# A hybrid pooling and state-space layer: state-space blocks projected first, the scan in two halves of groups, tables on VectorE, the output projection in two passes

## The reference, cut to what matters

```python
h = rmsnorm(x) * (1 + sc1) + sh1                  # sc1, sh1, g1, sh2, sc2, g2: silu(cond) @ w_ada
proj = h @ w_in                                   # 1024 -> 512 pooling channels, 512 state-space channels
pool_out = [(window_mean(u_g, w) - u_g) @ pool_w[g] for w in (2, 4, 8, 16)] * pool_scale
# state space: 32 groups of 16 channels, 64 complex states, one scan in each direction
bu = einsum("gnp,blgp->blgn", b_bar, u);  h_t = a_bar * h_{t-1} + bu_t
y = gelu(D * u + Re(C_f h_f) + Re(C_b h_b));  ssm_out = y * sigmoid(y @ w_glu)
x = x + g1 * (concat(pool_out, ssm_out) @ w_out)
x = x + g2 * (square(relu(norm(x) @ w_mlp1)) @ w_mlp2)
return rmsnorm(x), final context states
```

## Time and profile before

| | |
|---|---|
| median of three runs | 1408.06 us (1408.01 to 1409.33) |
| the profiled execution | 1408.4 us, span from first to last instruction 1406.6 us |
| TensorE | 1265.9 us busy, 90% of the span, mean granted clock 0.951 |
| VectorE | 909.6 us busy |
| GpSimd | 625.9 us busy |
| ScalarE | 306.4 us busy |
| chain that ended last | TensorE 73%, GpSimd 12%, VectorE, DMA and ScalarE 3% each |

### The profile page before, as it was taken

How to read it: one execution, slowest core, us unless ns; L and a number is a source line. 1 busy time by engine, 2 the same in 40 slices (tenths; PEclk the granted TensorE clock), 3 DMA queues, 4 the chain that set the end, 5 groups by cost and what they waited for, 6 DMA issues and landing times.

```text
span 1406.6 us, 18516 instructions
## 1 busy us (share of the span) xinstructions
PE 1265.9 (90%) x6399; PEld 1062.3 (76%) x6399; DVE 909.6 (65%) x1238; ACT 306.4 (22%) x595; POOL 625.9 (44%) x458
## 2 busy tenths in 40 slices
PE   3869997847788898899999999999999999999995
PEld 0269894104467786799899889989988998998893
DVE  1778689999944765884664565466456545645648
ACT  2462324002122311641011001101101110110113
POOL 1100412992103378524733653573375356337436
PEclk9879998877989999999999999999999999999998
DMA  8711366530484511020110111011001001101003
GB/s 208 257 30 31 112 132 106 185 119 1 75 254 69 173 30 46 16 90 23 53 60 30 30 60 45 15 60 60 29 30 60 31 28 60 59 17 43 30 0 134
DMA packets 82834, 101.63 MB, mean 72 GB/s; under 512 B 31974, under 2 KB 66442, under 8 KB 82412
## 3 DMA queue, kind: packets, MB, share of 16 engines
q1 hardware_dynamic: 62360, 85.59, 20.8%
q0 software_dynamic: 3136, 12.06, 3.3%
q10 hardware_dynamic: 17300, 3.48, 1.3%
HBM read 89.53 MB, written 9.49 MB: 70 GB/s over the span
## 4 chain that ended last, share of the span: by engine, by line
PE 73%; POOL 12%; DVE 3%; DMA 3%; ACT 3%; SPq 2%; issue 2%; ACTq 1%; POOLq 0%; DVEq 0%
PE bank L1088 21%; PE bank L1090 21%; PE bank L1089 21%; POOL acc L459 4%; POOL from_state L437 2%; POOL acc L469 2%; DMA raw<-in_w_ada 2%; POOL ca_tmp L434 2%; POOL from_state L432 2%; SPq L350 1%; PE bank L1101 1%; ACT h_tile L506 1%; PE bank L1205 1%; PE bank L1231 1%; ACTq L483 1%
## 5 line engine op out<-in xcount | busy, mean ns | idle before, releaser
L469 POOL TENSOR_TENSOR acc<-acc,gated 128x512 f32<-128x512 f32 x288 | 401.8, 1395 | 391.7 <-DVE gated L1052 352.7
L1088 PE MATMUL bank<-x_hi,w_hi 128*128 128x384 f32 x992 | 332.8, 335 | 0.0
L1089 PE MATMUL bank<-x_lo,w_hi 128*128 128x384 f32 x992 | 332.2, 335 | 0.0
L1090 PE MATMUL bank<-x_hi,w_lo 128*128 128x384 f32 x992 | 332.1, 335 | 0.0
L1052 DVE TENSOR_TENSOR gated<-bank,gate_b 128x512 f32<-128x512 f32 x288 | 194.4, 688 | 117.8 <-PE bank L1090 96.3
L1088 PE MATMUL bank<-w_hi,f_hi 128*128 128x512 f32 x576 | 224.4, 390 | 1.4 <-DVE w_lo L1033 0.8
L1090 PE MATMUL bank<-w_hi,f_lo 128*128 128x512 f32 x576 | 224.4, 390 | 0.0
L1089 PE MATMUL bank<-w_lo,f_hi 128*128 128x512 f32 x576 | 224.4, 390 | 0.0
L1042 DVE TENSOR_TENSOR f_tmp<-relu 128x384 f32<-128x384 f32 x96 | 65.5, 682 | 210.9 <-ACT relu L716 210.5
L716 ACT ACTIVATE relu<-bank 128x384 f32<-128x384 f32 x96 | 47.2, 493 | 649.0 <-PE bank L1090 647.3
L1088 PEld LDWEIGHTS bank<-x_hi,w_hi 128*128 128x128 f32 x992 | 186.8, 188 | 0.7 <-issue 0.2
(11 more groups left out here) (237 smaller groups left out, 1500.6 us busy)
## 6 DMA issues: line engine op xcount, KB each, us to landing
raw<-in_w_mlp SPq DMA_DIRECT2D x64, 512.0 KB, 3.6
raw<-in_w_ada SPq DMA_DIRECT2D x48, 512.0 KB, 5.0
x_tile<-in_x_sample POOLq DMA_DIRECT2D x8, 512.0 KB, 8.4
raw<-in_w_in SPq DMA_DIRECT2D x8, 512.0 KB, 4.0
raw<-in_w_out SPq DMA_DIRECT2D x8, 512.0 KB, 7.0
acc<-in_x_sample SPq DMA_DIRECT2D x1, 4096.0 KB, 13.5
out<-acc SPq DMA_DIRECT2D x8, 512.0 KB, 2.6
inv_count_b<-in_inv_count POOLq DMA_DIRECT2D x4, 576.0 KB, 4.4
```

The lines of the kernel that those rows point to most:

```text
L469: GP.tensor_tensor(a, a, BT[i % 4][:], ALU.add).then_inc(s.acc, 1)
L1088: mm(out, sh_, mh, start=first, stop=False)
L1089: mm(out, sh_, ml, start=False, stop=False)
L1090: return mm(out, sl, mh, start=False, stop=last)
```

## The change

- The input projection takes the four state-space blocks first (`IN_MB`), then the pooling blocks. The 32 groups are two halves of 16. The states of the first half are made behind the third block (VectorE evacuates every second pair), those of the second half behind the projection. The chunks keep the context's columns beside the latents', so their transfers are half as many.
- `to_state` and `from_state` are built on VectorE, eight calls each of three operations on 1024 elements. The transposition of the `to_state` blocks is spread over the projection (`WB_AT`).
- The scan runs once for each half; the seven single steps at the top become three folds with steps of 1, 2 and 4 (two more powers). Between the steps of the first scan VectorE splits weights; between those of the second it gates the blocks of the first output pass.
- The pooling windows run on VectorE between the two scans, in one padded buffer that ScalarE fills (`pad`), with the latents' and the context's sums in one operation up to the last level.
- A unit of conditioning is four matmuls of 256 columns, each on its own 32 rows of PSUM, and the bias comes as a ninth unit of each part. Parts 4 and 5 are spread over the first output pass.
- The output projection has two passes of four input blocks: pooling channels beside the second scan, state-space channels behind the GLU.
- The store of the outputs goes out in four parts, and `acc` is loaded in four.

Of the lines taken out none is shown below; they are the ones described in the section before.

```diff
+GB = G // 2
+KK_AT = 5
+WB_AT = {(1, 0): (0, 1), (1, 1): (2, 3), (1, 2): (4, 5), (2, 0): (6, 7),
+         (3, 0): (8, 9), (3, 1): (10, 11), (3, 2): (12, 13), (4, 0): (14, 15)}
...
+    W_OUT1, W_GLU, W_OUT2, W1 = N_IN, N_IN + N_HALF, N_IN + N_HALF + N_GLU, N_IN + 2 * N_HALF + N_GLU
...
+    IN_MB = [4, 5, 6, 7, 0, 1, 2, 3]
...
+        def load_u(b):
+            for i in range(2):
+                sp.wait_ge(uds[2 * b + i], 16)
+            ud = UD[b * GB * SP:(b + 1) * GB * SP, :].rearrange("(g p) t -> p g t", p=SP)
+            for j in range(L):
+                sp.dma_start(U[b][j * SP:(j + 1) * SP, :, :], ud[:, :, j * CH:(j + 1) * CH]).then_inc(u_in[b], 16)
...
+        def store_y(b, h):
+            sp.wait_ge(s.y_ev, 8 * b + 4 * (h + 1))
+            g0 = b * GB + 8 * h
+            for j in range(L):
+                sp.dma_start(yd[:, g0:g0 + 8, j * CH:(j + 1) * CH], Y[b][j * SP:(j + 1) * SP, 8 * h:8 * h + 8, :])\
+                  .then_inc(yd_w[b], 16)
...
+        for g, q in enumerate((s.yr0, s.yr1, s.yr2)):
+            for k in range(4):
+                dst = YR[:, k, :]
+                if g < 2:
+                    sp.dma_start(lat_j3(dst[:, g * TG:(g + 1) * TG]), yds[:, k, 3 * g:3 * g + 3, 0:CL]).then_inc(q, 16)
+                else:
+                    sp.dma_start(lat_j3(dst[:, 2 * TG:LAT]), yds[:, k, 6:8, 0:CL]).then_inc(q, 16)
+                    sp.dma_start(dst[:, LAT:T].rearrange("p (j c) -> p j c", c=CC), yds[:, k, :, CL:CH]).then_inc(q, 16)
...
+        load_counts(2)
+        turn_local(0)
+        load_counts(3)
...
+        for i in range(18):
+            if i in (0, 6, 10):
+                gp.wait_ge((s.acc_in0, s.acc_in1, s.acc_in2)[(0, 6, 10).index(i)], 16)
+            if i == 16:
                 gp.wait_ge(s.acc_ctx_in, 16 * L)
+            add_gated(i, BT3[i % 3])
+            if i == KK_AT:
+                turn_local(1)
...
+            if i == 2:
+                act.wait_ge(s.wbt, 8)
+                for p_ in range(0, 16, 2):
+                    states_out(p_)
...
+        pad(0)
+        for hf in range(2):
+            ada_row(2, hf)
+        pad(1)
+        kernels_out(0)
+        for hf in range(2):
+            ada_row(3, hf)
+            ada_col(3, hf)
+        pad(2)
+        for i in range(8):
+            y_out(0, i)
+        pad(3)
...
+        act.wait_ge(s.mix_pool, NG)
+        act.wait_ge(s.yd_w0, 16 * 2 * L)
+        kernels_out(1)
+        for hf in range(2):
+            ada_row(4, hf)
+            ada_col(4, hf)
+        for hf in range(2):
+            ada_row(5, hf)
+        for i in range(8):
+            y_out(1, i)
...
+        def to_state(b, d, h):
+            gs = slice(b * GB + 8 * h, b * GB + 8 * h + 8)
+            q0 = d * G + gs.start
+            out = WB[b][:, d, 8 * h:8 * h + 8, :].rearrange("n g (j p) -> n g j p", p=SP)
+            powers = [t_[:, L - 1::-1, q0:q0 + 8] if d == 0 else t_[:, 0:L, q0:q0 + 8] for t_ in (PR, PI)]
+            pr, pi = (t_.rearrange("n e q -> n q e").unsqueeze(3).to_broadcast([P, 8, L, SP]) for t_ in powers)
+            b1, b2 = (t_[:, q0:q0 + 8, :].unsqueeze(2).to_broadcast([P, 8, L, SP]) for t_ in (B1, BY))
+            tmp = TPQ[:, 0:8 * P].rearrange("n (g j p) -> n g j p", g=8, p=SP)
+            tt(tmp, b2, pi, ALU.mult).then_inc(s.dve, 1)
+            tt(out, b1, pr, ALU.mult).then_inc(s.dve, 1)
+            count[0] += 2
+            dve.wait_ge(s.dve, count[0])
+            tt(out, out, tmp, ALU.add).then_inc(s.wbt, 1)
...
+        def scan(b, between):
+            hb = H[b]
+            step = [0]
+
+            def folded(ins):
+                then(ins)
+                between(step[0])
+                step[0] += 1
...
+            for k in range(4):
+                folded(fold(b, 0, 4 * k, 4, slice(1, CH - 2, 2), slice(2, CH - 1, 2)))
+            for k in range(2):
+                folded(fold(b, 1, 8 * k, 8, slice(2, CH - 5, 4), slice(4, CH - 3, 4)))
+            folded(fold(b, 2, 0, GB, slice(4, CH - 11, 8), slice(8, CH - 7, 8)))
+            folded(fold(b, 3, 0, GB, slice(8, CL - 23, 16), slice(16, CL - 15, 16)))
+            then(V.memset(hb[:, :, :, CL], 0.0))
+            for i in range(3):
+                w = 16 << i
+                folded(fold(b, 4 + i, 0, GB, slice(0, CL - 15 - w, 16), slice(w, CL - 15, 16)))
+            folded(fold(b, 3, 0, GB, slice(0, CL + 1, 16), slice(8, CL + 9, 16)))
+            folded(fold(b, 2, 0, GB, slice(0, CH - 7, 8), slice(4, CH - 3, 8)))
+            for k in range(2):
+                folded(fold(b, 1, 8 * k, 8, slice(0, CH - 3, 4), slice(2, CH - 1, 4)))
...
+        to_state(0, 0, 0)
+        to_state(0, 0, 1)
+        split_lo(2, FIRST_IN + 2)
+        to_state(0, 1, 0)
+        to_state(0, 1, 1)
+        power_chain()
+        split_lo(3, FIRST_IN + 3)
         for d in range(2):
+            for h in range(2):
+                to_state(1, d, h)
+        split_lo(4, FIRST_IN + 4)
+        for p_ in range(1, 16, 2):
...
+        def beside_first(k):
+            if k in (1, 5, 11):
+                w = 5 + (1, 5, 11).index(k)
+                split_lo(w, FIRST_IN + w)
+
+        scan(0, beside_first)
+        dve.wait_ge(s.c_ready, 16)
+        for d in range(2):
+            for h in range(2):
+                from_state(0, d, h)
+        for gi in range(4):
+            pool_window(gi)
...
+        dve.wait_ge(s.y_mm, 8)
+        for h in range(2):
+            from_state(1, 0, h)
         for g in range(NG):
             cols = slice(g * TG, (g + 1) * TG)
             dve.wait_ge(s.mix_hi, g + 1)
             tt(XL[:, 0:4, cols], POOL[:, :, cols], XH[:, 0:4, cols].bitcast(F32), ALU.subtract).then_inc(s.mix_pool, 1)
+            if g == 0:
+                for w in range(2, 4):
+                    split_lo(W_OUT1 + w, FIRST_OUT1 + w)
+        for h in range(2):
+            from_state(1, 1, h)
+        dve.wait_ge(s.st_act, 24)
+        dve.wait_ge(s.gb1_in, 16)
+        dve.wait_ge(s.yd_w0, 16 * 2 * L)
+
+        def beside_second(k):
+            if k < 18:
+                gate_out(k)
+
+        scan(1, beside_second)
...
+        def ada_unit2(u):
+            part, k = 2 + u // (KB + 1), u % (KB + 1)
+            n = FIRST_ADA2 + u if u < N_ADA2 else FIRST_ADA4 + u - N_ADA2
+            raw_landed(pe, n)
+            if k == 0 and part == 4:
+                pe.wait_ge(s.gates_w, 16 * 2)
+            if k == 0 and part == 5:
+                pe.wait_ge(s.acts, 2)
+            cv = COL[:, 0:16].rearrange("p (a k) -> p a k", a=2)[:, :, k % KB]
+            for j in range(4):
+                o = BANK[4 + part % 2][32 * j:32 * j + 2, 0:256]
+                if k < KB:
+                    last = mm(o, cv, RAW[n % 4][:, 256 * j:256 * j + 256], start=(k == 0), stop=False, skip_group_check=True)
+                else:
+                    last = mm(o, ONE[:], RAW[n % 4][0:1, 256 * j:256 * j + 256], start=False, stop=True, skip_group_check=True)
+            last.then_inc(s.ada_used, 1)
...
+            for r in range(N_HALF):
+                k, w = (0 if o_ < 18 else 4) + r, w_slot(w0 + r)
+                last = three(BANK[o_ % 4][:], (XH[:, k, t * P:(t + 1) * P], XL[:, k, t * P:(t + 1) * P]),
+                             (WH[w][:, n * 512:n * 512 + 512], WL[w][:, n * 512:n * 512 + 512]), r == 0, r == N_HALF - 1)
...
+        pe.wait_ge(s.w_split, W_OUT1 + N_HALF)
+        for o_ in range(18):
+            pe.wait_ge(s.mix_pool, o_ // 2 // 3 + 1)
+            out_block(o_, W_OUT1)
+            if o_ == KK_AT:
+                for i in range(8):
+                    kernel_pair(1, i)
+            ada_unit2(N_ADA2 + o_)
+            if o_ == KB + 1:
+                ada_turn(4)
+        for i in range(8):
+            y_pair(1, i)
...
```

More of the change, by code:

```diff
@@ L133, in build @@
[L133 to L138, removed]
-    INV = at("inv_count_b", [P, T], R_W + 16 * KBYTE + 9536)
-    Y = at("y_chunks", [P, G, CH], R_U)
+    H0S = at("first_states", [P, Q], R_C + 10336)
+    PROJ = [at(f"proj{i}", [P, L, CH], R_U + 9216 + i * 4608) for i in range(2)]
@@ new lines, in power_chain @@
+        def power_chain():
+            then(V.tensor_copy(AQ[0:N, :], PI[0:N, L, :]))
+            then(ts(AQ[N:P, :], PI[N:P, L, :], -1.0, None, ALU.mult))
+            for i in range(6):
+                (sr, si), (dr, di) = powers[-1], (AR_[i][:], AI_[i][:])
+                then(tt(dr, sr, sr, ALU.mult))
+                then(tt(di, si, si, ALU.mult))
+                then(tt(dr, dr, di, ALU.subtract))
+                then(tt(di, sr, si, ALU.mult))
+                then(ts(di, di, 2.0, None, ALU.mult))
+                powers.append((dr, di))
@@ new lines, in states @@
+        def states(i):
+            b, d, g0 = i // 16, i % 2, 2 * (i % 16 // 2)
+            if i % 16 == 0:
+                pe.wait_ge(s.wb_ready, 8 * (b + 1))
+                pe.wait_ge(u_in[b], 16 * L)
+            if i == 16:
+                pe.wait_ge(s.in_ev, 24)
+            if 4 <= i < 16:
```

(34 more changed lines are left out.)

1045 lines of the change are left out of this document (513 added, 532 removed).

## The result

The changed kernel takes 1422.32 us (median of four runs, 1419.88 to 1423.99), the kernel before 1408.2 (four runs by now; it was 1408.06 with three). The ratio is 1.0097, 95% interval 1.0079 to 1.0116: slower by 1%. I had forecast 1388 and a range from 1366 to 1412. The profiled execution of the changed kernel took 1423.66 us, its span is 1421.6.

A forecast was written before the change was run, and what follows sets the result against it. The path was taken as projection, scan, round trip, GLU, output projection, followed along VectorE. Span 1406.6 + 31.7 − 20.5 − 32.5 + 1.5 = 1386.8 us, so a time of 1388; range 1366 to 1412.

The forecast's parts named there:

- table operation: Building `to_state` and `from_state` on VectorE: 1.23 us for each operation on 1024 elements.
- GELU to end of GLU: Store, reload through DRAM and GLU behind the last GELU: 44.3 us instead of 64.9, a gain of 20.5.
- second pass: Output projection of state-space channels behind the GLU: 61.6 us instead of 94.1, a gain of 32.5.
- last GELU 464: VectorE's path through first scan, tables, windows and second scan: last GELU ends at 464 us, against 432.35 before.
- break-even: Last GELU at 484 us, 20 us later than forecast, where the change would neither gain nor lose.
- rival 4: Window waits 28, meetings 23 and issues 1.3 make gains and losses cancel: 1400 to 1408 us; chance 0.08.
- meetings: Second scan: VectorE's folds lengthened by GpSimd's additions beside them; 18 times 0.9, 16 us (8 to 23).
- the rule's price: Second scan, shared SBUF port: an addition of 1.3 us costs VectorE all 1.3; the sum would be 7 us more.
- The tail: Behind the last GELU: gains of 20.5 us (round trip, GLU) and 32.5 (second pass), loss of 1.5 (feed-forward start).
- The first: Window waits short and a meeting only 0.46 us: 13 and 8 us less, 1367 to 1375; chance 0.20.
- The second: VectorE's table operations run at the price of strided folds, 1.98 us each: 24 us more, 1412; chance 0.12.
- The third: TensorE becomes the bound of the second scan through a low clock; at 0.65 the end is 1425 us; chance 0.10.

The follow-up runs named there:

- first experiment: Changed kernel with the second half's output pairs given PSUM banks in the order the gates free them; 1416.25 us, ratio to the kernel before 1.006.

## Why the prediction was wrong

The sign was wrong, and most of its mechanisms were right. Forecast and measured, by its steps (us):

| step | forecast | measured |
|---|---|---|
| table operation | 1.23 | 1.22 |
| first scan | 149 to 244 | 152.9 to 249.7 |
| wait ahead of the third window, its start | 20 us, 294 | 23.8 us, 303.3 |
| windows end | 326 | 337.0 |
| second scan starts | 350.5 | 367.2 |
| last fold | 460 | 481.9 |
| last GELU | 464 | 493.5 |
| GELU to end of GLU | 44.3 | 46.0 |
| second pass | 61.6 | 62.4 |
| hidden blocks behind it | 3.6 | 5.1 |

**The step that failed is VectorE's path to "last GELU 464".** It gave no term to two waits, for the channel maps (6.05) and for banks that the first output pass still holds (a part of 11.5 instead of 4.5), and its 20 for the third window was too small. The sum stood 20 us from its own break-even, and was 29.5 short, in five places, none of them over 8:

1. 5.7 by the end of the first scan: VectorE comes to the state pairs 1.3 later than forecast, waits 2.5 for TensorE at three of them, and one fold operation is 0.9 longer than its like. The last 1.0 I can't name.
2. 5.3 more at the windows. I had ScalarE's order and the loads right, and the columns at 293; they came at 298.8 to 302, as TensorE waits 2.9, 2.3, 3.0 and 5.8 us for the loads of the last four units, 14.0 in all.
3. 5.7 ahead of the second scan: a wait for `x_hi`, which needs the twelve channel maps. I had given them no term: before, they lay beside the scan. Here ScalarE empties them from 337.4 to 351.0, all behind the windows, although TensorE had four done by 324. A weight split stands ahead of them in ScalarE's order, and it waits 15.4 us for the fourth window (the row at 335.48).
4. 5.2 in the second scan: 2.4 is a gate that waits for TensorE, 0.7 the eighteenth gate, of which I had counted 17 ahead of the last fold, and the rest fold operations somewhat longer than alone (near 440, 1.3 for 576 elements against 1.12).
5. 7.5 at the output pairs: from last fold to last GELU are 11.5 instead of 4.5 (and the forecast's own sum was 464.5). I let the pairs follow the folds as these finish. They wait for banks that the first pass holds up to its last two gates, and then run partly at 1.2 GHz. With the better bank order 3.5 of it is gone (first experiment); the last gate's bank and the clock are the rest.

Most of it is of one kind: what a step waits for in another queue once its cover is gone. I had looked for that at the windows and the splits, and left it out for the maps and the banks. Each looked small beside a path of 460 us, and I gave the case that small losses add up (rival 4) eight in a hundred, with 1400 to 1408 for it. Of the three losses it names only the window waits came (28.4 for its 28); the meetings were 16, not 23. Small losses did add up, but mostly ones that it does not name.

**The terms of VectorE's own work held.** Tables, windows (44.4), gates and folds (82.6 + 81.3 forecast, 168 measured) are right to 3%. A meeting was forecast at 0.9 and measured at 0.9 in the mean (0.8 to 1.05). The Trainium skill (SBUF — State Buffer, on the shared port pair) has the later instruction wait for the whole of the other; the trace agrees in kind. The addition at 460.20 lasts 1.83, which holds the fold operation of 0.76 beside which it began, and the next fold operation is 0.95 longer. The 1.3 that I named as the rule's price is more than what then is left of the addition, some 1.07. But GpSimd's table in the kernel before cost the scan 38.7 us where I had expected 10 to 14: the price of such meetings for a whole scan is not read off a few pairs of rows.

**The tail held too**, 5.3 us worse than forecast in the profiled execution: 1.7 in the round trip, 0.8 in the pass, 1.5 ahead of the hidden blocks, which also start at 0.50 of the clock (1.2 GHz) behind a wait of 3.8, and the rest in the loop.

**The rivals.** The first (short window waits, cheap meetings) is out at 28.4 and 0.9. The second (tables at the strided price) is out at 1.22. The third (TensorE as the bound) did not come: it was granted 0.83 from 367 to 482, near my limit of 0.8, but only one gate waits for it. Its units were far shorter than the 1.77 that I took the earlier trace rows: four in 1.91 us, 0.48 each. The Trainium skill (TensorEngine Tiling (Array Packing), column tiling) has narrow products on different column strips run at once; the trace agrees, 0.48 against the 0.45 that I had estimated by it. From 1.77 and 0.48 that is 23 us for 18 units, in a stage that TensorE does not bound.

**Why the change is slower than before at all**: it moved the pooling windows (44 us), the first output pass's gates (29 with the meetings), `from_state` (29) and weight splits with `x_lo` (13) onto VectorE's one chain, cut the folds in halves (24), and hung that chain on the order of ScalarE and TensorE (45 us of waits in five places). That is 184. The earlier start (62), the table off GpSimd (39), the shorter way from the last fold to the last GELU (22) and the shorter tail (46) give 169, all but 15. The waits are no part of the idea: with a good part of them mended it ends at 1384.6. That this is near the forecast of 1388 is partly luck, as that version has orders of maps and banks that the forecast did not think of.

Still open: why executions of the changed kernel differ by up to 4 us, why one fold operation of the first scan takes 2.1 us instead of 1.2, and how much is to be had by getting the `local` copies out of the loads' way, which I did not try.

## What to carry to other kernels

When work is moved onto an engine's serial chain, price not only its operations but, for each moved piece, what it now waits for in the other in-order queues and in banks still held by the stage before; a row of before cannot price a wait that was covered there. Where a forecast rests on one long sum, compare the distance to break-even with the number of terms in it: ten terms that each can only be late by 3 to 7 us are a likely case, not the last one. And long operations of GpSimd that read SBUF beside VectorE's two-input operations are paid for on VectorE: here a table of 48 of them cost 38.7 us of a scan, and 18 additions 16.

## What the runs showed of the hardware

- VectorE doing an addition of 512 columns itself (0.72 with its gap) is cheaper than letting GpSimd do it beside the folds (0.9 of delay in the mean): 3.2 us of the scan for 18, and 5.2 of the kernel's time.
- Beside folds of 1120 elements GpSimd's operations on 16 elements took 2.1 us, beside steps of 64 elements 0.22, and the folds were no longer than alone. With 512 elements each, the same 48 operations made the scan 38.7 us longer.
- TensorE's granted clock was 1.00 from 463 to 471, in those products and the first pair, and 0.56 from 477 to 482, behind a wait of 3.6 us (2.4 GHz and mostly 1.2 GHz). 14 us of products ahead of the pairs bought nothing.
- Halving 16 folds and seven single steps cost VectorE 21.5 us: an operation on 568 elements takes 0.75 against 1.34 for 1136, and one on 32 elements 0.20 to 0.22 against 0.26 for 64.
